# A two-layer hybrid block on one core: split the second branch's projection, cut the mask into pieces, move small steps between engines

## The reference

```python
for l in range(2):
    hx = modulate(rmsnorm(x_lat, norm1_g[l]), sh1, sc1)      # and hc from x_ctx
    z = hx @ w_in[l]                                          # 4608 columns for the mixers, 4096 for the gates
    branches = [pool_x, diff_x, sgu_x, na_x]                  # four mixers, 512 columns each
    # diff_x: differential attention, its output rmsnorm'ed per head
    # na_x: neighbourhood attention, scores + bias inside a window, masked outside it
    gsig = sigmoid(gates.reshape(T, 4, 1024))
    proj = einsum('tie,ied->tid', branches, w_br[l])
    x_lat = x_lat + g1 * (sum_i(gsig * proj) @ w_out[l])
    hx2 = modulate(rmsnorm(x_lat, norm2_g[l]), sh2, sc2)
    x_lat = x_lat + g2 * ec_moe(hx2, router_w[l], moe_w1[l], moe_w3[l], moe_w2[l])   # 16 experts
return rmsnorm(x_lat, final_g)
```

## Time and profile before

| what | us |
|---|---|
| median of three runs | 2088.93 |
| the profiled execution | 2085.78 |
| its span, first to last instruction | 2084.0 |
| mean granted TensorE clock | 0.943 |
| PE busy | 1817.4 (87%) |
| DVE busy | 697.5 (33%) |
| ACT busy | 435.1 (21%) |
| POOL busy | 115.4 (6%) |

### The profile page before, as it was taken

How to read it: one execution, slowest core, us unless ns; L and a number is a source line. 1 busy time by engine, 2 the same in 40 slices (tenths; PEclk the granted TensorE clock), 3 DMA queues, 4 the chain that set the end, 5 groups by cost and what they waited for, 6 DMA issues and landing times.

```text
span 2084.0 us, 24722 instructions
## 1 busy us (share of the span) xinstructions
PE 1817.4 (87%) x9928; PEld 1076.3 (52%) x9928; DVE 697.5 (33%) x1117; ACT 435.1 (21%) x760; POOL 115.4 (6%) x157
## 2 busy tenths in 40 slices
PE   6999999999999899999999799999997665656565
PEld 3878756666787433333333488977895121112111
DVE  3272354643343412222212444457555010101001
ACT  3212333332222210000000332344333000000000
POOL 2070000000000100000000232000000000000000
PEclk9999999999999999999999999999999778787777
DMA  9423233344437699999999853343679999999996
GB/s 313 138 78 103 88 107 108 105 133 130 152 122 290 270 412 422 422 422 422 421 422 422 254 156 93 112 152 127 213 227 390 398 421 422 421 422 422 421 421 282
DMA packets 233132, 565.53 MB, mean 271 GB/s; under 512 B 12152, under 2 KB 159760, under 8 KB 183888
## 3 DMA queue, kind: packets, MB, share of 16 engines
q1 hardware_dynamic: 230736, 557.73, 69.8%
q0 software_dynamic: 1760, 4.40, 1.2%
q10 hardware_dynamic: 544, 2.10, 0.3%
HBM read 563.11 MB, written 1.07 MB: 271 GB/s over the span
## 4 chain that ended last, share of the span: by engine, by line
PE 70%; DMA 22%; DVE 4%; issue 2%; SPq 1%; ACT 1%; POOL 0%; POOLq 0%; ACTq 0%; DVEq 0%
PE PS L764 45%; PE PS L1201 17%; DMA nab<-in_moe_w 13%; DMA e_wr<-in_moe_w 7%; PE PS L1152 2%; PE PS L814 2%; PE PS L939 1%; DMA ring<-in_w_mod 1%; PE PS L961 1%; SPq L741 1%; PE PS L1179 0%; PE PS L1162 0%; DMA ring<-in_w_in 0%; DVE arena L1763 0%; PE PS L1085 0%
## 5 line engine op out<-in xcount | busy, mean ns | idle before, releaser
L764 PE MATMUL PS<-hTr,wr 128*128 128x512 f32 (+1 forms) x2688 | 517.4, 349 | 6.6 <-DVE hTr L1691 6.6
L764 PEld LDWEIGHTS PS<-hTr,wr 128*128 128x128 f32 x2688 | 429.9, 191 | 74.9 <-issue 7.3
L1201 PE MATMUL PS<-arena 128*32 128x512 f32 (+1 forms) x960 | 306.2, 710 | 86.3 <-DMA nab<-in_moe_w 43.0
L1639 DVE TENSOR_TENSOR wr<-ring,wr 128x1024 fp32r<-128x1024 f32 x152 | 188.0, 1237 | 225.4 <-ACT wr L1269 225.2
L1269 ACT ACTIVATE wr<-ring 128x1024 fp32r<-128x1024 f32 x152 | 160.9, 1059 | 299.4 <-PE PS L764 274.9
L1201 PE MATMUL PS<-e_h,arena 128*64 128x512 f32 (+1 forms) x624 | 164.0, 691 | 51.0 <-DMA arena<-in_moe_w 45.2
L1201 PE MATMUL PS<-arena,e_h 128*64 128x512 f32 (+1 forms) x576 | 171.3, 706 | 30.2 <-DMA nab<-in_moe_w 15.0
L1201 PEld LDWEIGHTS PS<-arena 128*32 128x32 f32 (+1 forms) x960 | 83.3, 140 | 215.5 <-issue 210.6
L764 PE MATMUL PS<-wr,hTr 128*128 128x512 f32 x816 | 187.9, 391 | 4.8 <-DVE hTr L1893 2.6
L764 PEld LDWEIGHTS PS<-wr,hTr 128*128 128x128 f32 x816 | 151.9, 188 | 38.2 <-DVE wr L1639 3.4
L2063 DVE TENSOR_TENSOR x<-x,PS 128x512 f32<-128x512 f32 x80 | 55.0, 688 | 241.7 <-PE PS L764 241.7
(11 more groups left out here) (186 smaller groups left out, 1819.7 us busy)
## 6 DMA issues: line engine op xcount, KB each, us to landing
arena<-in_moe_w SPq DMA_DIRECT2D x192, 1024.0 KB, 18.2
e_h<-in_moe_w SPq DMA_DIRECT2D x90, 1024.0 KB, 18.9
ring<-in_w_in SPq DMA_DIRECT2D x136, 512.0 KB, 4.0
e_wr<-in_moe_w SPq DMA_DIRECT2D x64, 1024.0 KB, 20.5
ring<-in_w_mod SPq DMA_DIRECT2D x92, 512.0 KB, 5.4
nab<-in_moe_w SPq DMA_DIRECT2D x32, 1024.0 KB, 21.7
ring<-in_w_br SPq DMA_DIRECT2D x64, 256.0 KB, 4.9
ring<-in_w_out SPq DMA_DIRECT2D x16, 512.0 KB, 3.4
```

The lines of the kernel that those rows point to most:

```text
L764: return nc.tensor.matmul(o, a, b, start=first, stop=last)
L1201: ins = nc.tensor.matmul(PS[g * R:(g + 1) * R, bank + h, :], src[:, k, g * R:(g + 1) * R], space[:, kk * D + h * 512:kk * D + (h + 1) * 51 ...
L1639: nc.vector.tensor_tensor(wr[:, j % 2, 1, :], ring[:, slot, :], wr[:, j % 2, 0, :].bitcast(f32), ALU.subtract).then_inc(w_lo.sem, 1)
```

## The change

It has these parts.

- Mask: POOL adds it in eight operations of 128x384 in place of one of 128x3072; only the last one signals.
- Means: for the norm in front of a layer, the last norm, and the output norms of the differential attention, the mean with the epsilon is now a DVE `tensor_scalar` (`mean_square`, and one after the `reduce_sum`), and POOL does the power alone. The norm in front of the experts and the gating norm stay as they were.
- Modulation columns: a new event "cols" stands after the first half of the gates of unit 16. The eight chunks of the gate part move to units 17 to 24.
- Sums: ACT rounds the first two merged sums ahead of the second chunk of `w_out`; `EARLY` is 2.
- Second branch: units 8 to 15 too are projected in three passes (`SPLIT` = 8). The branch is split over the first four events of unit 7, its high part into the tile of `dk`; the pieces of `w_br` from unit 8 on are split one unit ahead, in units 8 to 15 into the tile of `dv`. The differential branch's high part moves to the tile of `nk`. The gates' spreading DMA waits for unit 15's projection too.

The diff, cut to its core:

```diff
-        todo, start, at_ = (first, 0, n) if n < half else (second, len(first), n - half)
+        todo, start, at_ = (first, 0, n) if n < half else (second, len(first), n - half - 1)
...
-    events = [("gates", 0)] + mods[:-1] + [("gates", 1)] + mods[-1:] + [("proj", None)]
+    cols = [("cols", None)] if u["n"] == NBR * KD // 2 else []
+    events = [("gates", 0)] + cols + mods[:-1] + [("gates", 1)] + mods[-1:] + [("proj", None)]
...
-        split_hi = {1: 4, 3: 5}
+        split_hi = {2: 4, 1: 5, 3: 4}
-        wbr = nab_r[:, 0:2048].rearrange("p (a b c) -> p a b c", a=2, b=2)
+        wbr_early = arena_r[:, 6, :].rearrange("p (a b c) -> p a b c", a=2, b=2)
+        wbr_late = nab_r[:, 0:2048].rearrange("p (a b c) -> p a b c", a=2, b=2)
...
+                sync.wait_ge(*projs.at(l, HALF))
...
-                            if n < HALF:
+                            if n < SPLIT:
                                 br = take(("br", l, n))
                             else:
-                                pe.wait_ge(*wbr_lo.at(l, n - HALF + 1))
-                                pe.wait_ge(*branch_lo.at(l, 4 * (u["p"] - 1)))
+                                pe.wait_ge(*wbr_lo.at(l, n - SPLIT + 1))
+                                pe.wait_ge(*branch_lo.at(l, 4 * u["p"]))
...
+                        elif what == "cols":
+                            mod_post(l, done + len(mod_steps(l)[0]) - 1)
...
-                    b, k = MERGE_ORDER[2 + t // 4], t % 4
-                    act.wait_ge(*pv.at(l, nb))
-                    act.wait_ge(*at_act.at(l, tr_n["act"]))
-                    act.wait_ge(*o_norm.at(l, NG[l]))
+                    b, k = MERGE_ORDER[1 + t // 4], t % 4
+                    if t < 4:
+                        act.wait_ge(*w_dve.at(l, counts["dve"]))
+                        act.wait_ge(*scores.at(l, nb // 2))
+                    else:
+                        act.wait_ge(*pv.at(l, nb))
...
+                    act.wait_ge(*pv.at(l, nb // 2 if n < HALF else nb))
+                    nc.scalar.activation(wbr(n)[:, 0, :], ring[:, slot, 0:512], ACT.Copy).then_inc(wbr_hi.sem, 1)
...
-                        for t in range(4):
+                        for t in range(4, 8):
                             branch_high(t)
-                        projection_high(HALF)
-                    for what, arg in unit_events(u):
+                    for e, (what, arg) in enumerate(unit_events(u)):
+                        if n == SPLIT - 1 and e < 4:
+                            branch_high(e)
...
-                    if n >= HALF:
+                    if n >= SPLIT - 1:
                         projection_high(n + 1)
...
+                    if k == 1:
+                        high(l, NW + NM + 1)
...
-                pool.tensor_tensor(tb, tb, cst[:, C_MASK:C_MASK + GRID_W].unsqueeze(1).broadcast_to([128, 48, GRID_W]),
-                                   ALU.add).then_inc(bias_masked.sem, 1)
+                for h in range(8):
+                    th = tb[:, 6 * h:6 * h + 6, :]
+                    ins = pool.tensor_tensor(th, th, cst[:, C_MASK:C_MASK + GRID_W].unsqueeze(1).broadcast_to([128, 6, GRID_W]),
+                                             ALU.add)
+                ins.then_inc(bias_masked.sem, 1)
...
-                    pool.wait_ge(*o_ss.at(l, g + 1))
-                    inverse_root(oss[:, 0:4], oms, orstd, 4, 1.0 / 128, o_rstd.sem)
+                    pool.wait_ge(*o_mean.at(l, g + 1))
+                    pool.tensor_tensor(orstd, oms, half, ALU.pow).then_inc(o_rstd.sem, 1)
...
+            def mean_square(nn, s):
+                dve.wait_ge(*sq_done.at(nn, 2 * s + 2))
+                c = slice(2 * s, 2 * s + 2)
+                nc.vector.tensor_scalar(ms[:, c], ss[:, c], 1.0 / D, EPS, ALU.mult, ALU.add).then_inc(mean_done.sem, 1)
...
                 if l:
+                    mean_square(2 * l, 0)
                     normalise(2 * l, 0)
+                    mean_square(2 * l, 1)
                     normalise(2 * l, 1)
...
-                EARLY = 4
+                EARLY = 2
...
+                        if n == SPLIT - 1 and e < 4:
+                            branch_low(e)
...
+                        elif what == "cols":
+                            mod_columns(l, l, 1, 3 if l == 0 else 1)
```

More of the change, by code:

```diff
@@ L401, in build @@
         sq_done = signal("sq_done", *NN)
+        mean_done = signal("mean_done", norms[0][2], 0, norms[2][2], 0, 2)
         rstd_done = signal("rstd_done", *[n for _, _, n in norms[:4]], 2)
@@ L442, in build @@
         o_square = signal("o_square", *[n // 2 for n in NG])
-        o_ss = signal("o_ss", *[n // 2 for n in NG])
+        o_mean = signal("o_mean", *[n // 2 for n in NG])
         o_rstd = signal("o_rstd", *[n // 2 for n in NG])
@@ L1547, in inverse_root, with roots @@
                 pool.tensor_tensor(root[:, 0:n], mean[:, 0:n], half[:, 0:n], ALU.pow).then_inc(ready, 1)
+            def roots(nn, n_streams):
+                for s in range(n_streams):
+                    pool.wait_ge(*mean_done.at(nn, s + 1))
+                    c = slice(2 * s, 2 * s + 2)
+                    pool.tensor_tensor(rstd[:, c], ms[:, c], half[:, 0:2], ALU.pow).then_inc(rstd_done.sem, 1)
             def norm_roots(nn, n_streams):
@@ L1567, in _ @@
                     pool.dma_start(bm[:, :, :], A["gate_bias"][l]).then_inc(gate_bias_loaded[l], 16)
-                norm_roots(2 * l, 2)
+                roots(2 * l, 2)
                 if l == 0:
@@ L1899, in _ @@
                     if n == HALF:
-                        for t in range(4):
+                        for t in range(4, 8):
                             branch_low(t)
-                        projection_low(HALF)
                     events = unit_events(u)
-                    for (what, arg), after in zip(events, events[1:] + [(None, None)]):
+                    for e, ((what, arg), after) in enumerate(zip(events, events[1:] + [(None, None)])):
+                        if n == SPLIT - 1 and e < 4:
+                            branch_low(e)
                         if after[0] == "att":
@@ L2109, in _ @@
                     .then_inc(fin_scaled, 1)
+                dve.wait_ge(*sq_done.at(4, m + 1))
+                nc.vector.tensor_scalar(ms[:, m:m + 1], ss[:, m:m + 1], 1.0 / D, EPS, ALU.mult, ALU.add)\
+                    .then_inc(mean_done.sem, 1)
+            for m in range(2):
                 dve.wait_ge(*rstd_done.at(4, m + 1))
```

64 lines of the change are left out of this document (36 added, 28 removed).

## The result

| | before | after |
|---|---|---|
| median of the runs beside each other | 2087.32 us (4) | 2071.3 us (4) |
| profiled execution | 2085.78 us (span 2084.0) | 2070.7 us (span 2068.9) |

The ratio is 0.9926, 95% interval 0.9907 to 0.9945: 15.4 us faster (11.5 to 19.4). Two more sets of five runs of the same kernel gave medians of 2073.72 (0.9940, 0.9924 to 0.9956) and 2070.99 (0.9926, 0.9913 to 0.9939), so the change is worth some 14 us. The forecast was 9.4. The sign and most terms were right, and about a third of the gain was not in the sum.

A forecast was written before the change was run, and what follows sets the result against it. PE was taken to bound the mixers and DMA the expert stages; 7.8 + 2.2 + 2.9 - 1.1 - 1.3 - 1.1 = 9.4 us off the 2088.93 median gave 2079.5 us, range 2073.5 to 2087.

The forecast's parts named there:

- Mask: Layer 0, behind POOL's mask add: PE's wait goes whole, 2.2 us gained, bounds 0 to 2.2; layer 1, 0.
- Three passes: Units 8 to 15: shorter projections gain 5.4 us in layer 0 and 2.4 in layer 1, sum 7.8.
- piece d: Layer 0, from the tanh of unit 8 to that of unit 31: forecast -7.1 us.
- late softmax: Rival, chance 0.18: softmax slack in units 8 on is thinner than read, 5 to 6 us lost, time 2085.0.
- Unit 7: Second branch's roundings delay the softmax in unit 7: 1.1 us lost in layer 0, 1.3 in layer 1.
- Piece c: Layer 0, from weight remainder 24 to the tanh of unit 8: forecast +1.1 us.
- Columns: Unit 16's waits go, 2.9 us gained (2.4 to 3.3), with 0.45 lost to branch 1's last remainder in layer 1.
- Start of layer 1: First norm of layer 1: the mean queues behind DVE's expert adds, 1.1 us lost, bounds 0.8 to 1.4.
- Rounding the sums: Before the output projection: PE waits for its own seven increments, so 0 us gained, bounds 0 to 1.3 a layer.
- the rival of the rounding: Rival, chance 0.12: rounding was PE's wait before the output projection; both waits of 1.3 us go, time 2076.9.
- piece h: Layer 1, from the tanh of unit 17 to the last weight remainder: forecast 0.
- piece e: Layer 0, from the tanh of unit 31 to the last expert weights landed: forecast 0.

## Why the prediction was right or wrong

**Three passes: right.** 0.68 us a unit in layer 0: piece d of this part alone is -5.24, forecast 5.4. PE had one gap of 0.18 us in units 8 to 15, so the late softmax (rival, 2085.0) didn't happen.

**Unit 7: right in layer 0, too small in layer 1.** 1.1 forecast in layer 0. Piece c scatters (-1.1 to +0.4 in the six traces without the three passes, -0.1 to +1.5 in the nine with them in unit 7), its means differ by 1.2. In layer 1, 1.3 forecast: the wait for the output norm grew by 0.87, and unit 8's projection waits another 0.87, which the term didn't have; 1.7 together, 1.5 of it between the tanh of units 7 and 8.

**Columns: right in kind, at the lower bound in size.** 2.9 forecast, 2.4 measured alone (1.6 + 0.8): the new wait in layer 1 is 0.83 to 0.88, not 0.45. It comes even where branch 1's remainders weren't moved, so the reason on record for it is not the whole one.

**Mask: mechanism right, size too small.** The term took the wait alone, 2.2 us. It left out what the clock does behind a wait. The piece is worth 2.48 us where the clock holds and 4.07 where it falls, and it fell in four of seven traces: 3.4 on average, 1.2 above the term.

**Start of layer 1: the step failed.** The delay is there as forecast, 1.0 us at the normalisation. "PE's transposes, the tiles and the first chunk with it" was wrong, because I took PE's speed as fixed: its clock pattern shifted and gave the microsecond back. Forecast -1.1, measured 0. That the mean is what shifts it is not shown: two kernels without it have the same pattern.

**Rounding the sums: half failed.** "Seven increments, not the sums, are what PE waits for" holds, and the rival of the rounding is out. But I priced the moved step on PE alone. Its other customer is the ring: the remainder frees the slot for which SyncE waits with all expert loads behind it. In layer 0 that is worth nothing (slots full), in layer 1 1.3 us where the clock holds and, with what lies behind the last landing, up to 2.4. In run times neither undoing it (0.4 us slower) nor doing it alone (2087.09 against 2086.65) shows this; it is read from the landmarks only.

**Left out altogether.** PE's two waits for modulation weights in layer 1, 1.9 and 2.0 us in the traces of before and 0 to 0.2 in those of after. They are 1.8 us of gain, of which piece h shows 1.2 because of the chunk moved into it:

```profile
1509.93 0.64 PE L814 MATMUL PS<-ring,cond 128*32 128x256 f32 x8 [0.83 <-DMA ring<-in_w_mod]
1526.19 0.64 PE L814 MATMUL PS<-ring,cond 128*32 128x256 f32 x8 [1.03 <-DMA ring<-in_w_mod]
```

They are 0.2 us with the three passes alone, 0.6 with the rounding, 0.9 with the mean, 1.3 with the mask and 1.8 with the columns alone. Which shift decides stays open. And piece e, 0.8 to 1.4 us of routing, which goes with the granted clock there.

Together: 9.4, + 1.2 for the mask, + 1.1 at the start of layer 1, + 0.9 (e), + 1.8 (modulation weights), + 2.2 (i), less 1.5 in c, d and g (columns and unit 7 above), is 15.1. The range, 2073.5 to 2087, missed it because each bound was drawn around a wait or an instruction, and none around the clock or the DMA queue: of what the sum missed, some 3.2 us are the clock's (mask, start of layer 1, e) and up to 4.0 the queue's (modulation weights, i). That the clock pattern came out in the change's favour in layer 0's routing and at the start of layer 1 was luck. The median of before, 2085.4 to 2087.3 in later sets, was also 1.6 to 3.5 us below the 2088.93 that I started from.

## What to carry to other kernels

Cut both traces at common landmarks and compare lengths: most pieces repeat to a few tenths of a microsecond where run times scatter by three. Check that the same work lies between the landmarks in both kernels, and compare the granted clock of a piece before a gain in it is put down to a part. Price a wait of TensorE with the clock behind it, and a moved step at each of its readers: what frees a slot may have a whole stream queued behind it, which pays only if that stream isn't stopped later by full slots. When TensorE has thin work around a change, a microsecond won or lost there may be undone by where the half-clock stretch falls, so don't add it to the sum at face value.

## What the hardware showed that I had not expected

A wait of 2.16 us, with PE busy without gaps before and behind, was followed by a half-clock stretch that cost 1.6 us in four of seven traces. The mean granted clock over 20 us of layer 0's routing was the same in every trace of one kernel (0.74 twice, 0.83 three times), while small edits elsewhere moved it from one value to the other; 2.5 us slices within it repeated to 0.01 in the kernel before and differed by up to 0.15 in the changed one. An operation of 7.16 us on POOL cut into eight takes 10.20 us, about 1.0 us a piece alone and up to 2.1 beside VectorE. Seven semaphore increments in PE's own queue stand for 1.3 us in front of the next matmul; on POOL's queue they cost PE nothing.
